# A two-block transformer kernel: latent attention on a ring of single PSUM banks, 528-token products cut at 256, padded rows, and three steps reordered

## The reference

```python
h = concat([meta, x])                                       # 528 tokens
for l in range(2):
    h = h + 0.5 * swiglu(rmsnorm(h, ffn1_norm[l]), ...)     # 1024 -> 2816 -> 1024
    u = rmsnorm(h, mix_norm[l])
    if l == 0:
        h = h + pool_mixer(u, pool_w[l], pool_scale[l])
    else:
        h = h + mla_attention(u, w_dq, q_latent_norm, w_uq, w_o, k_nope, k_rope, v)
    h = h + 0.5 * swiglu(rmsnorm(h, ffn2_norm[l]), ...)
    if l == 0:       # keys and values come from a latent of 256 features
        shared = mla_shared_kv(rmsnorm(h, kv_in_norm), w_dkv, kv_latent_norm, w_uk, w_uv)
x = rmsnorm(h, final_norm)[:, 16:]

def mla_attention(...):   # 8 heads; blocks of 128 queries; chunks of 64 keys, chunk-causal
    cq = rmsnorm(h @ w_dq, q_latent_norm)
    s = (qn @ k_nope + qr @ k_rope) * scale; s = where(mask, s, min)
    p = softmax(s); o = p @ v                                # v: 64 features a head
    return o @ w_o

# second block
u = rms_norm(x, mix_norm_g)
q, k, v, conv and gate inputs = split(u @ w_in)
q = rms_norm(q per head, q_norm_g); k = rms_norm(k per head, k_norm_g)
y_a = stick_breaking_attention(q, k, v) @ w_attn_out
y_b, y_c = two convolution branches; merged = sum of sigmoid gates * y
x = x + merged @ w_o
x = x + swiglu(rms_norm(x, ffn_norm_g) @ w_ffn_in) @ w_ffn_out
```

## Time and profile before

| | us |
|---|---|
| median of 3 runs | 2459.85 |
| lowest, highest | 2456.71, 2471.16 |
| the profiled execution | 2462.93 |
| its span on the core | 2461.1 |
| mean granted TensorE clock | 0.997 |
| TensorE busy | 2425.6 (99%) |
| VectorE busy, ScalarE busy | 1542.4 (63%), 1443.6 (59%) |
| latent attention, first scores to the first output product | 75.80 |

### The profile page before, as it was taken

How to read it: one execution, slowest core, us unless ns; L and a number is a source line. 1 busy time by engine, 2 the same in 40 slices (tenths; PEclk the granted TensorE clock), 3 DMA queues, 4 the chain that set the end, 5 groups by cost and what they waited for, 6 DMA issues and landing times.

```text
span 2461.1 us, 40079 instructions
## 1 busy us (share of the span) xinstructions
PE 2425.6 (99%) x16262; PEld 2214.3 (90%) x16262; DVE 1542.4 (63%) x2162; ACT 1443.6 (59%) x1901; POOL 285.9 (12%) x336
## 2 busy tenths in 40 slices
PE   8999999999999999999899999999999999999999
PEld 7999999999999899998679999977777788999998
DVE  7756656867566867565557676653777433676664
ACT  7547466555467565467565564755765465654743
POOL 1001010110111110111001110111001111110100
PEclk9999999999999999999999999999999999999999
DMA  7758593675687585688236866976556888575855
GB/s 210 173 141 197 146 223 87 172 197 136 155 205 183 144 223 127 166 212 197 54 69 155 214 154 164 232 170 141 123 119 143 189 182 195 126 186 156 205 152 149
DMA packets 245063, 404.49 MB, mean 164 GB/s; under 512 B 12384, under 2 KB 170720, under 8 KB 244880
## 3 DMA queue, kind: packets, MB, share of 16 engines
q0 software_dynamic: 47808, 174.08, 38.2%
q1 hardware_dynamic: 197072, 227.85, 29.0%
HBM read 225.73 MB, written 2.10 MB: 93 GB/s over the span
## 4 chain that ended last, share of the span: by engine, by line
PE 59%; DVE 4%; ACT 1%; DMA 1%; issue 1%; DVEq 0%; ACTq 0%; SPq 0%
PE ps L645 30%; PE ps L769 21%; PE ps L716 1%; PE ps L1036 1%; PE ps L1070 1%; PE ps L948 1%; PE ps L1083 1%; PE ps L935 1%; DVE wS L1680 1%; PE ps L1060 1%; DMA raw<-in_w_ffn_in 1%; DVE wL L1689 1%; DVE m L1995 0%; PE ps L1075 0%; DVE h L1998 0%
## 5 line engine op out<-in xcount | busy, mean ns | idle before, releaser
L769 PE MATMUL ps<-xbH,wH 128*128 128x256 f32 (+1 forms) x2800 | 786.5, 281 | 2.3 <-ACT kept L1301 1.1
L769 PE MATMUL ps<-xbH,wL 128*128 128x256 f32 (+1 forms) x2800 | 786.5, 281 | 0.0
L769 PE MATMUL ps<-xbL,wH 128*128 128x256 f32 (+1 forms) x2800 | 786.4, 281 | 0.0
L604 POOL DMA_DIRECT2D wL<-raw x332 | 285.7, 861 | 2147.9 <-ACT wL L1161 2120.6
L769 PEld LDWEIGHTS ps<-xbH,wH 128*128 128x128 f32 x2800 | 526.0, 188 | 4.0 <-issue 2.1
L769 PEld LDWEIGHTS ps<-xbL,wH 128*128 128x128 f32 x2800 | 526.1, 188 | 0.4
L769 PEld LDWEIGHTS ps<-xbH,wL 128*128 128x128 f32 x2800 | 525.9, 188 | 0.0
L1161 ACT ACTIVATE wL<-raw 128x1024 fp32r<-128x1024 f32 x332 | 349.9, 1055 | 214.9 <-PE ps L645 177.8
L1175 ACT ACTIVATE wH<-wS 128x1024 fp32r<-128x1024 f32 x200 | 212.5, 1062 | 418.5 <-DVE wS L1680 407.3
L1179 ACT ACTIVATE wH<-raw 128x1024 fp32r<-128x1024 f32 x375 | 392.5, 1047 | 77.4 <-PE ps L645 65.8
L645 PE MATMUL ps<-aH,wH 128*128 128x264 f32 (+1 forms) x1232 | 350.8, 331 | 2.6 <-DVE var L2073 1.9
(11 more groups left out here) (300 smaller groups left out, 3181.1 us busy)
## 6 DMA issues: line engine op xcount, KB each, us to landing
wL<-raw POOLq DMA_DIRECT2D x332, 512.0 KB, 5.7
raw<-in_ffn_w_gate SPq DMA_DIRECT2D x88, 512.0 KB, 5.1
raw<-in_ffn_w_up SPq DMA_DIRECT2D x88, 512.0 KB, 5.7
raw<-in_ffn_w_down SPq DMA_DIRECT2D x88, 512.0 KB, 5.6
raw<-in_w_in SPq DMA_DIRECT2D x56, 512.0 KB, 4.3
raw<-in_w_ffn_in SPq DMA_DIRECT2D x44, 512.0 KB, 5.1
raw<-in_w_ffn_out SPq DMA_DIRECT2D x22, 512.0 KB, 5.4
raw<-in_w_o SPq DMA_DIRECT2D x12, 512.0 KB, 5.4
```

The source lines that it names most:

```text
L604: nc.gpsimd.dma_start(wL[:, u % RING, :], raw[:, UNITS[u].raw % RAW, :], accum_op=ALU.add).then_inc(lo_in[u % RING], 16)
L769: ins = nc.tensor.matmul(ps[:, 2 * s + j, 0:TH], lhs, rhs, start=p in (1, 5, 2) and k == q == 0, stop=p in (2, 3, 4) and k == KP - 1 and q ...
```

## The change

- **Latent attention.** S, T, V and the queries Q take single banks from a ring of six (banks 2 to 7; two banks for the scores of i = 3, whose 528 columns need them); T's meta keys gather for a whole head in bank 0 or 1. Meta keys come first in the scores, one product of 144, 272 or 400 columns (16 + 512 for i = 3). `pmT` and `vmeta` become fp32r with 96 rows (high, low, high part of 16 rows each, 32 apart), and V's meta product one fp32r matmul. V follows two heads behind, ahead of the scores of i = 1. ScalarE copies T before it does the exponential; per head it copies the meta rows once ("high") and once more ("again"), and VectorE makes the low part ("low"). Q0 and Q1 are made ahead, Q2 to Q7 among the heads 0 to 4. `oH` and `oL` have a place of their own. The first three of four feature blocks of `wo` 0 to 2 ("W", 27 of 96 matmuls) come between the last transposes and V's.
- **The cut.** Products and statistics of 528 tokens are cut 256 + 272 and written next to each other across the bank border, so that readers read one run.
- **Rows.** The rows of `xbH`, `xbL` for 528 tokens lie 1088 bytes apart instead of 1056.
- **Head sums.** `head_stats(n - 2)` stands inside pair n, (2) ahead of v and (3) in it; VectorE clears `hscale` earlier, and scales x2 by `final_norm` from tile 4 on, two each.
- **Latent variance.** `latent_scales("kv")` comes ahead of the multiplication that waits for the SiLU.
- **Kept copy.** In the first gating after a stage, ScalarE's weight conversion of p = 1 comes one copy later.

The diff, cut to its core:

```diff
+CUT = SEQ // 2
+XROW = {T1: 272, SEQ: SEQ // 2}
...
+MROW, KMETA = 2 * NMETA, 6 * NMETA
...
+LAG = 3
+META_BANKS, MLA_BANKS = (0, 1), (2, 3, 4, 5, 6, 7)
+LAST_BANKS = {("V", NH - 2, 0): 7, ("T", NH - 1, 2): 4, ("T", NH - 1, 3): 5, ("V", NH - 1, 0): 3}
+WO_AHEAD = 3
+
+
 def mla_order():
 
-
-
     steps = [(h, i) for h in range(NH) for i in range(NT)]
-    order = []
-    for s in range(len(steps) + 3):
-        if s < len(steps):
-            order.append(("S",) + steps[s])
-        if s >= 3:
-            hd, i = steps[s - 3]
-            if i == 2 and hd:
-                order.append(("V", hd - 1, 0))
-            order.append(("T",) + steps[s - 3])
-    return order + [("V", NH - 1, 0)]
+    queries = {(0, 0): 2, (0, 1): 3, (1, 1): 4, (2, 1): 5, (3, 1): 6, (4, 1): 7}
+    order = [("Q", 0, 0), ("Q", 1, 0)]
+    for n, (hd, i) in enumerate(steps):
+        order.append(("S", hd, i))
+        if i == 0 and hd >= 2:
+            order.append(("low", hd - 2, 0))
+        elif i == 1 and hd >= 2:
+            order.append(("o", hd - 2, 0))
+        if n:
+            order.append(("p",) + steps[n - 1])
+        if n >= LAG:
+            order.append(("T",) + steps[n - LAG])
+        if i == 3 and hd >= 1:
+            order.append(("high", hd - 1, 0))
+        elif i == 0 and hd >= 2:
+            order += [("again", hd - 2, 0), ("V", hd - 2, 0)]
+        if (hd, i) in queries:
+            order.append(("Q", queries[hd, i], 0))
+    last = NH - 1
+    return order + [("p", last, 3), ("low", last - 1, 0), ("T", last, 1), ("again", last - 1, 0), ("V", last - 1, 0),
+                    ("T", last, 2), ("o", last - 1, 0), ("T", last, 3), ("high", last, 0), ("low", last, 0),
+                    ("again", last, 0), ("W", 0, 0), ("W", 1, 0), ("V", last, 0), ("o", last, 0), ("W", 2, 0)]
...
+            blocks[f] = tuple(place(f"xb{b}{f}", [P, 7, KP, XROW[T]], F32R, b_at)[:, :, :, 0:T // 2]
+                              for b, b_at in (("H", h_at), ("L", l_at)))
...
+        oH = place("oH", [P, NH // 2, SEQ], F32R, zs)
+        oL = place("oL", [P, NH // 2, SEQ], F32R, zs + NH // 2 * SEQ * 4)
...
+        vmeta = place("vmeta", [P, NH * DV], F32R, zv + NT * NH * DV * 4)
+        pmT = place("pmT", [P, 2, SEQ], F32R, zv + (NT + 1) * NH * DV * 4)
...
-            return ps[:, 2 * s:2 * s + 2, 0:HALF] if T == T1 else ps[:, 2 * s, 0:T]
-
-        def like(ap, T):
-            return pairs(ap) if T == T1 else ap
+            return flat(s)[:, CUT:CUT + T] if T == T1 else ps[:, 2 * s, 0:T]
...
+        def scores(hd, i):
+            b = C.slot.get(f"mla:S{hd}:{i}", 0)
+            w = NMETA + (i + 1) * P
+            return ps[:, b:b + (w + BANK - 1) // BANK, :].rearrange("p b n -> p (b n)")[:, 0:w]
...
-                parts = [(0, HALF), (HALF, T1)] if T == T1 else [(0, T)]
+                parts = [(0, CUT), (CUT, T1)] if T == T1 else [(0, T)]
...
+                        to = CUT if T == T1 and c == 0 else 0
+                        ins = nc.tensor.matmul(ps[:, 2 * s + c, to:to + b - a], lhs, r[:, a:b],
...
+            def banks(name, reader, n=1, last=None):
+
+                if last is None:
+                    if n == 2:
+                        ring[0] += ring[0] % 2
+                    b = MLA_BANKS[ring[0] % len(MLA_BANKS)]
+                    ring[0] += n
+                else:
+                    b = last
+                for x in range(b, b + n):
+                    clear(x)
+                    readers[x] = reader
+                C.slot[name] = b
+                return ps[:, b, :], ps[:, min(b + 1, 2 * SLOTS - 1), :]
...
-                    nc.tensor.matmul(b1[:, 0:NMETA], q, kcat[:, hd, 0:NMETA], start=True, stop=True)
-                    ins = nc.tensor.matmul(b0[:, BANK - (i + 1) * P:BANK], q,
-                                           kcat[:, hd, NMETA:NMETA + (i + 1) * P], start=True, stop=True)
+                    if w > BANK:
+                        nc.tensor.matmul(b1[:, 0:w - BANK], q, kcat[:, hd, BANK:w], start=True, stop=True)
+                    n = min(w, BANK)
+                    ins = nc.tensor.matmul(b0[:, 0:n], q, kcat[:, hd, 0:n], start=True, stop=True)
...
+                    transposed(meta_bank(hd)[:, i * P:(i + 1) * P], prob[:, n, 0:NMETA], P)
                     for j in range(i + 1):
-                        transposed(b0[:, j * P:(j + 1) * P], src[:, w0 + j * P:w0 + (j + 1) * P], P)
-                    ins = transposed(b1[0:NMETA, 0:P], src[:, BANK:BANK + NMETA], P)
+                        ins = transposed(b0[:, j * P:(j + 1) * P], prob[:, n, NMETA + j * P:NMETA + (j + 1) * P], P)
...
-                    ins = nc.tensor.matmul(b0[:, :], vmeta[:, cols], pmT[:, hd % 2, :], start=False, stop=True,
+                    pe.wait_ge(act_done, at("act", f"mla:h{hd}"))
+                    pe.wait_ge(dve_done, at("dve", f"mla:l{hd}"))
+                    ins = nc.tensor.matmul(b0, vmeta[0:KMETA, cols], pmT[0:KMETA, hd % 2, :],
+                                           start=False, stop=True,
...
+            pe.wait_ge(dve_done, at("dve", f"ol{NH - 1}"))
+            for d in range(KD):
+                if d >= WO_AHEAD:
+                    group(f"wo:{d}", None, TURN[d % SLOTS])
+                else:
+                    owner[TURN[d]] = "dve", f"rd:wo:{d}"
+                done(wo_part(d, range(NH // 2 - 1 if d < WO_AHEAD else 0, NH // 2)), f"wo:{d}")
...
+            def mpair(u, stage, n, kwait=None, stats_of=None):
                 for e in range(2):
+                    if e and stats_of is not None:
+                        head_stats(stats_of)
...
-                else:
-                    head_stats(n - 1)
...
+            head_stats(2)
...
-                    if not (part == 0 and p == 2):
+                    if not (part == 0 and p == 2) and not (p == 1 and kept_back):
...
+                    if waiting:
+                        exponential(*waiting)
+                        waiting = None
+                elif what == "V":
...
+                elif what == "high":
+                    fn(nc.scalar.activation(pmT[0:NMETA, hd % 2, :], ps[0:NMETA, META_BANKS[hd % 2], :], ACT.Copy),
+                       f"mla:hi{hd}")
+                elif what == "again":
+                    act.wait_ge(act_done, at("act", f"mla:hi{hd}"))
+                    fn(nc.scalar.activation(pmT[2 * MROW:2 * MROW + NMETA, hd % 2, :], pmT[0:NMETA, hd % 2, :],
+                                            ACT.Copy), f"mla:h{hd}")
...
+                        if f == 2 and part == 0:
+                            latent_scales("kv", RKV, T1)
...
-                    if f == 2 and (part, it, p) == (0, 1, 4):
-                        latent_scales("kv", RKV, T1)
...
+                elif what == "low":
+                    on_act(f"mla:hi{hd}")
+                    if hd >= 2:
+                        on_pe(f"mla:V{hd - 2}:0")
+                    do(V.tensor_tensor(pmT[MROW:MROW + NMETA, hd % 2, :], ps[0:NMETA, META_BANKS[hd % 2], :],
+                                       f32(pmT[0:NMETA, hd % 2, :]), ALU.subtract), f"mla:l{hd}")
...
-                do(V.scalar_tensor_tensor(x2[:, f, :], x2[:, f, :], gcol("final_norm", f), ss[:, 0:SEQ],
-                                          ALU.mult, ALU.mult))
                 if f:
                     square_low(f - 1)
+                if f >= NH // 2:
+                    for d in (2 * f - NH, 2 * f - NH + 1):
+                        do(V.scalar_tensor_tensor(x2[:, d, :], x2[:, d, :], gcol("final_norm", d), ss[:, 0:SEQ],
+                                                  ALU.mult, ALU.mult))
```

218 lines of the change are left out of this document (123 added, 95 removed).

## The result

The changed kernel takes 2434.39 us (median of 4 runs, 2425.67 to 2440.01) against 2463.24 (4 runs, 2456.71 to 2471.16) for the kernel before: a ratio of 0.9879, 95% interval 0.9855 to 0.9904, 1.2% faster. Measured again later, 5 runs gave 2436.24 against 2458.15, ratio 0.9911 (0.9889 to 0.9933). The forecast was 2422.5 with a range of 2402 to 2437: the time is in the range, and the gain is 22 to 29 us where 37 were forecast. The profiled execution took 2432.20 with a span of 2430.0, 31.1 less than before.

What follows compares the result with a forecast made beforehand. TensorE, busy 99% of the span, was taken as the bound. Terms -16.2 - 6 - 4 - 6.5 - 3.5 - 1.1 = -37.3, with 3.1 more off the profiled 2462.93, gave 2422.5 us; range 2402 to 2437.

Steps and rivals of the forecast that it cites:

- rival 2: FFN products: time hangs on columns alone, so cut and padded rows give 0; -27.3 in all, 2432.5 us; chance 0.18.
- Latent attention: Latent attention stage: less TensorE work, waits and low clock, 59.6 us against 75.80, -16.2 us (bounds -10 and -19).
- per-head wait: Latent attention heads: scores no longer wait for the exponential; all 5.1 us go.
- the tail: End of latent attention: 27 output products, 6.1 us, run before the last values and cover a 1.6 us wait.
- Products cut at 256: 528-token products: 1,152 pairs cut 256 + 272 instead of 264 + 264 run faster, -6 us.
- Rows of 1088 bytes: Products reading 264-column rows: the row step of 1056 bytes, not the column count, costs; -4 us.
- Head sums: Head sums of q and k: both waits, 3.7 us, and the low clock after them go; -6.5 us (bounds -3.7 and -7).
- Latent variance: Variance before FFN 2's first down product: TensorE's 1.9 us wait and 1.6 us of low clock go; -3.5 us.
- Kept copy: Kept copies behind ScalarE's weight conversions: two waits of 0.5 to 0.6 us go; -1.1 us.
- rival 3: 256-column levels turn: cut and rows at lower level, 2398 us; or an FFN changes level, 7.7 us either way; chance 0.14.
- The signs: Trace checks: stage near 60 us, heads 7.0 to 7.4 apart, exponential waits under 0.3, pairs 232 to 241 ns, gate/up under 121.

Runs made afterwards that it cites:

- meta_fp32: Changed kernel with V's meta product back in fp32 with one copy; first query to FFN 3 takes 98.75 us against 98.69.
- v_behind: Changed kernel with V and the copy ahead of it moved behind the scores of i = 1; first query to FFN 3 takes 102.59 us against 98.69.
- ring_of_four: Changed kernel with S, T, V and Q on four single banks instead of six; first query to FFN 3 takes 112.14 us against 98.69.
- cut_rows_back: Changed kernel with the cut back at 264 + 264 and rows at 1056 bytes; 504 gate and up products take 61.77 or 61.78 us against 61.21.
- order_back: Changed kernel with the reorderings of head sums, latent variance and kept copy undone; +7.5 us in all.
- queries_first_no_wo: Changed kernel with all eight queries ahead of the scores and no output products ahead of the last V; first query to FFN 3 takes 102.92 us against 98.69.
- after_again: Changed kernel once more, no edit; single runs 2432.83 to 2439.45 us, attention stage 98.75 us.
- meta_early: Changed kernel with meta rows' high part, low part and second copy handled earlier; 2433.55 us, ratio 0.9902 to the kernel before, first query to FFN 3 94.19 us.

## Why the prediction was right, and which of its steps failed

The measured medians, 2434.39 and 2436.24, lie in the range, but 12 to 14 us above the forecast of 2422.5 and within 3 us of the upper bound, nearer to the 2432.5 of rival 2. Set term by term, -15.6 (attention), -0.2 (cut), -3.4 (rows), -6.7 (head sums), -2.5 (variance) and -1.3 (kept copy) come to -29.7 where -37.3 were forecast, and 5.8 of the missing 7.6 are the cut. That the whole still fell in the range owes something to its width and something to luck, since two parts of the attention were missed in opposite directions.

**Latent attention: right in sum, wrong inside.** -15.6 against -16.2. The per-head wait of the scores for the exponential went, the tail was covered (2.7 us by the output products), and the head's work fell to 6.93 us busy, against 7.0. Over the whole stage TensorE's busy time fell by 104.62 - 93.28 = 11.3 us, where 7.8 of work and 1.5 of clock make 9.3; its idle time fell by 9.72 - 5.42 = 4.3, where 9.72 - 2.8 = 6.9 was forecast. The two misses, 2.0 and 2.6 us, nearly cancel, and that is luck. I had counted 0.63 us a head for the fp32r meta product; it takes 0.34 and not 0.23 us, and meta_fp32 shows the saving paid back in full by waits for its copies. VectorE, which I had at 5.75 us a head, is busy for 5.90 of 7.69. My text gave the end of the per-head wait to V standing ahead of the scores; v_behind makes V's place 3.9 us, and ring_of_four makes the fifth and sixth bank 13.4. These overlap, and no run divides the 15.6 among the parts.

**Products cut at 256: the step that failed.** I took -6 between two levels, on the ground that 256 columns run at 112.6 ns and 264 at 121.7. The pair is 241.5 against 241.0, and the same run of 288 is 35.19 us with the cut and 35.25 without: next to nothing. The comparison joined columns and level: a 256-column product beside a 272-column one, in FFN 0 and 1, is at the upper of its levels (118.3 ns to the next start), and the one of 272 takes 124.9, 6.6 more for 16 columns, where the full clock of 2.4 GHz gives 16/2.4 = 6.7. Here rival 2 was right. So was, for the sum of a cut, the linear rule of the Trainium skill ("TensorE: Matmul & The Clock Gate", section "Back-to-back issue gap"), which I had said the trace spoke against. An estimate by that rule, 528/2.4 + 5 = 225 ns for two products, is 16 ns under the 241.5 measured.

**Rows of 1088 bytes: right, -3.4 against -4.** The step of the rows costs, and not the count of columns, as the term had it; cut_rows_back takes a run back to 61.78, and 1072 lies between. Here rival 2, which gave the rows nothing, was wrong. Why a step costs isn't shown. The lower level that would have given -21.7 was never seen at 264 columns.

**Head sums: -6.7 against -6.5,** confirmed by order_back with +5.4 on the way back, where less of the low clock returned: 0.72 over 6 us from 1616, where the kernel before had 0.82 and 0.61 over 12 us from 1630.

**Latent variance: right mechanism, size depends on the level.** -2.5 against -3.5. In the kernel before, TensorE ran FFN 2's first iteration at the lower level (192 products in 22.00 us) and came early to a variance whose time VectorE sets: 1.9 us of wait and the low clock. In the changed kernel it ran at the upper (22.85 us) and would have waited 0.9. In queries_first_no_wo the first iteration was at 22.00 again, with the variance early, and iteration and down products took 64.61, against 67.82 before: -3.2 like with like, +0.95 at the other level.

**Kept copy:** -0.8 in FFN 4 (60.30 to 59.52), -0.1 in FFN 3 (58.08 to 57.96) and, at the same level, -0.4 in FFN 2 (59.90 to 59.52 in after_again), together -1.3 against -1.1. Right. In FFN 2 of the first execution, which began that run at the lower level, 0.4 us of the wait is left.

**Outside the sum.** Two things moved that the change doesn't touch. FFN 2's last two parts took the lower level, -4.5 us, as rival 3 had it as a possibility. And FFN 3's last down products with the 48 behind them took 46.16 us, since ScalarE waited 6.53 us for the first weights of the second block. Its squares stand behind that conversion, VectorE waited 2.77 us for them ahead of its next read of a bank, and TensorE waited for the banks (the 1.5 us of line 2085). The conversion in the first execution, the same place in the second execution of the changed kernel, and in the kernel before:

```profile
1562.07 1.06 ACT L1236 ACTIVATE wL<-raw 128x1024 fp32r<-128x1024 f32 x1 [6.53 <-DMA raw<-in_w_in]
```

```profile
1569.33 1.06 ACT L1236 ACTIVATE wL<-raw 128x1024 fp32r<-128x1024 f32 x1 [7.50 <-DMA raw<-in_w_in]
```

```profile
1585.03 1.06 ACT L1161 ACTIVATE wL<-raw 128x1024 fp32r<-128x1024 f32 x1 [2.01 <-DMA raw<-in_w_in]
```

The conversion begins 14.2 us after the down products do in the first (1562.07 - 1547.84) and 15.2 in the second (1569.33 - 1554.13), against 11.4 before (1585.03 - 1573.59). These 192 products took 46.2 to 47.2 us in six of the eight executions whose FFN 3 had the lower level, and 44.1 in the other two (the kernel before and meta_early) and in all six at the upper. What delays the transfer there stays open; that a faster FFN 3 leaves it less time is argued, not shown.

Without levels and this wait the spans differ by -31.1 + 4.5 - 2.0 = -28.6, close to the medians' -28.9.

**The signs.** No wait before the head sums and none for the variance at FFN 2's first down product: both came. Gate and up products of 264 columns came at 120.5 in a quiet window and at 61.05/504 = 121.1 from run start to next start, on either side of the 121 that I named. The heads were to be 7.0 to 7.4 us apart, and were 7.4 to 7.6 from V to V where no query stands among them; the wait for the exponential was to stay under 0.3 us, and its longest is 0.6; the pair was to be 232 to 241 ns, and is 241.5 to 243.2, the value that I had called wrong. The stretch from the first scores to the last low output, 1149.52 to 1227.73, is 78.2 us; less 6.1 for output products and 54 x 0.229 = 12.4 for the six queries that moved into it, which the sign forgot, it is 59.7, as forecast.

## What to carry to other kernels

When a stage passes values between three engines, count buffers first: here six banks in place of four were worth 13.4 us, and each cheaper matmul or better place tried beside them at most 4.5. A cheaper product that needs extra copies should be priced with the wait of its user for the last copy, and the copies put a step earlier than they seem to be needed. Before a difference in matmul pitch is credited to a shape, look at the same shape in another execution of the same program.

## What the runs showed of the hardware that was not expected

Streams of 256-column fp32r products with one weight load each ran here at one of two distances from start to start, 113.3 or 117.8 ns (57.28 or 59.52 us for 504), at a granted clock of 1.00 in both. The level can differ between executions of one program and change within a run of 504. Seven such changes stand in the fourteen traces. Six fall at a hold of TensorE, where two starts lie 0.2 to 0.85 us apart (as in the changed kernel's 60.18, 113.3 ns before it and 117.8 behind); the seventh, in the 58.78 of meta_fp32, comes at product 168 with no hold (0.13 us). Other holds change nothing. The level held through the last two parts of FFN 2 and of FFN 3 in all but that case. Address steps of 1024 and 1056 bytes and a shift of 1024 did not choose it, and FFN 4 never had the lower one. Nothing tried here controls it, and it moves a whole time by 2.2 us for each of an FFN's later three parts. Streams of 264 columns showed only 61.21 to 61.78 us for 504, set by the step of their rows.
